# One inference step of a two-layer hybrid decoder: when the copies of the decode state are issued among the gathers of layer 1

## The chip, the cores and the metric

The kernel runs on one core of a Trainium2 chip. The metric is the device time of one execution in microseconds (us). Before the change the median of three runs is 816.68 us (815.47 to 819.44).

## The reference, cut to what matters

The step runs two layers for a prompt of 256 tokens and for eight samples of one new token each, all in float32. Layer 0 has differential attention and an indexer-sparse attention. Layer 1 has a native sparse attention (compressed blocks, selected blocks, a window of 512) and a dilated attention with three pairs of window and step, (128, 1), (512, 4) and (2048, 16). Each layer has one input projection, gates, one output projection and norms.

The outputs hold the results and the new state. For the samples, the state of the window attention and of the three dilated pairs is the old buffer shifted by the new row:

```
kd_all = [jnp.concatenate([d_bufs[2 * g], kd[g]], axis=1) for g in range(n_g)]
...
keep = lambda a, w: a[:, a.shape[1] - min(w, a.shape[1]):]
for g, (w, _) in enumerate(D_PAIRS):
    d_new += [keep(kd_all[g], w), keep(vd_all[g], w)]
```

Eight samples times eight such buffers are 64 blocks of old rows. They go unchanged from an input in device memory to an output in device memory, and no computation reads the copies. One sample's rows are 2048 KB for `d_k2` or `d_v2`, 1022 KB for `d_k1` or `d_v1`, 254 KB for `d_k0` or `d_v0`, and 255.5 KB for `c_win_k` or `c_win_v`.

## The kernel before, in words

Each engine follows one list of events, `ORDER` (built by `even_order` and `odd_order`), and does its own part of each event. TensorE (PE) carries out the projections (`rows`, `decode_rows`, lines 917 and 928), transposes (line 847), scores (1038), outputs of attention (1072) and the decode parts (1168, 1247, 1360, 1427). ScalarE (ACT) takes results out of PSUM, VectorE (DVE) does rotations, softmax parts and the decode products.

Transfers have two issuers. SyncE (SP, queue q1 in the profile) loads the weights, line 806, in chunks `win1_0` to `win1_13` for layer 1 and `wout1_0`, `wout1_1` for its output projection; the two halves of the buffer `ring` take them by turns, so that a chunk's load is issued when the one before last has been used. It also stores the new rows of prompt and samples (`out_p_...`, `out_s_... <-Z`, lines 2651 and 2657) and loads the post-norm weights (2619). At the end of layer 1 its program order is `wout1_0`, `wout1_1`, the post-norm weights, 16 stores of dilated values (line 2657), and at last `y`.

GpSimd (POOL, queue q0) issues what the decode side reads: gathers from the paged caches (`ak`, `av`, `bk`, `bv`, `ck`, `cv`; lines 814, 820, 826) and plain loads of the window and dilated state (`wk`, `wv`, `dk`, `dv`; line 810). Each waits until its buffer is free. In layer 1 their order is: ck0_0, ck0_1, ck1_0, ck1_1, dk0_0, cv_0, dk0_1, cv_1, cv_2, cv_3, dk1_0, dk1_1, wk0_0, wk0_1, dk2_0, wv_0, wv_1, dv0_0, dv0_1, dv1_0, dv1_1, dv2_0. A load `dk`, `wk`, `wv` or `dv` is 1024 KB. The last three `dv` loads lie in the half of `ring` that `win1_12` has left.

The 64 copies stand in one list, `MOVES`, in groups of four: the samples of `d_k2` and then `d_v2`, beside them those of `d_k0`/`d_v0`, `d_k1`/`d_v1`, `c_win_k`/`c_win_v`. POOL issues them too. After each gather or load it takes as many copies off the list as the table `MOVED_AFTER` (line 793) has under the gather's name, or else under its first two letters, or else none. What is left follows the last gather, `dv2_0`. A copy is cut into 16 pieces, one for each DMA engine, from memory to memory; nothing waits for it but the end of the program.

One wait matters at the end. The first product of layer 1's output projection is written into space from which SP's stores still read. So both ACT and DVE wait, ahead of that product (`out_rows` 1, 0, 0; lines 1635 and 2472), until every store of SP counted in `out0` has landed:

```
if (c, t) == (0, 0):
    ...
    eng.wait_ge(sem("post_in"), 16 * (l + 1))
    if l:
        eng.wait_ge(sem("out0"), 16 * (len(OUTS[0]) + len(OUTS[1])))
```

PE waits for `wout1_0` ahead of the same event. The last event chain after it is: ACT squares (1620), DVE weighting (2481), ACT copies of the transposed mix (1469), two products by PE of 16 matmuls each (917), the decode rows (928), the last product (917), norm and store.

Of the kernel before, what the change touches and what calls it, by code (L numbers as in the profile page):

```python
# [390 lines left out]
def build(nc, ins, outs):  # L391
    ctx = ExitStack()
    with ctx:
# [395 lines left out]
        for group in zip(moved("d_k2", 512) + moved("d_v2", 512), moved("d_k0", 512) + moved("d_v0", 512),  # L789
                         moved("d_k1", 512) + moved("d_v1", 512), moved("c_win_k", 128) + moved("c_win_v", 128)):  # L790
            MOVES += group

        MOVED_AFTER = dict(ak=1, ck=1, cv=1, dk=1, wk=1, wv=2, ak0_0=0, ak0_1=0, rows1_2=4, av7_1=3, bv_1=3, bv_3=4,
                           ck1_1=2, dk0_0=2, dk0_1=2, wk0_1=2, dk2_0=4, dk1_0=2, dk1_1=2, dv0_0=2, dv0_1=2)

        def stream(eng, name, parts):
            slot, before = place[name]
# [1872 lines left out]
        def _(pool):  # L2670
            pool.wait_ge(sem("index"), 5)
            moves = list(MOVES)
            for name, queue, parts in items:
                if queue == "pool":
                    stream(pool, name, parts)
                    for _ in range(MOVED_AFTER.get(name, MOVED_AFTER.get(name[:2], 0))):
                        if moves:
# [54 lines left out]
```

## Time and profile before

| what | value |
|---|---|
| median of three runs | 816.68 us |
| the profiled execution, its own time | 822.99 us |
| its span | 821.1 us |
| PE busy | 751.4 us, 92% |
| DVE busy | 426.0 us, 52% |
| ACT busy | 240.9 us, 29% |
| POOL busy | 165.0 us, 20% |
| DMA | 213.08 MB, mean 260 GB/s |
| q0 (POOL's transfers) | 142.55 MB |
| q1 (SP's transfers) | 69.62 MB |

Busy shares are of the span. The profiled execution's own time is 1.9 us above its span and 6.3 us above the median. In the profile MB are millions of bytes, KB are 1024 bytes. The letter q behind an engine's name means its sequencer, and L917 is line 917 of the kernel.

### The profile page before, as it was taken

To read this page: it belongs to the slowest core of one execution; us is meant where nothing else is said; L and a number is where in the kernel's file an instruction comes from. 1 tells how busy PE (TensorE), PEld (TensorE's weight loads), DVE (VectorE), ACT (ScalarE), POOL (GpSimd) and SP (SyncE) were. 2 spreads that over 40 slices of the span, in tenths; PEclk is the share of its full clock that TensorE was granted. 3 is DMA by queue.
4 is the path that set the end of the run, shared out by engine and by line. 5 is a ranking of instruction groups with operands and counts; after the bars stand their busy time and mean duration, and the time that the engine had idled before them with its cause. 6 is when DMAs were issued, how large, how long until landed. Compare 5 with 4: busy or idle time off the path is not lost.

```text
span 821.1 us, 12676 instructions
## 1 busy us (share of the span) xinstructions
PE 751.4 (92%) x4874; PEld 402.1 (49%) x4874; DVE 426.0 (52%) x958; ACT 240.9 (29%) x601; POOL 165.0 (20%) x202
## 2 busy tenths in 40 slices
PE   6989999998899799998999998899898799999896
PEld 4455545444454234433554554555554455555543
DVE  2114598999967989845244233231745425322214
ACT  6234233222213201122154323242330233232222
POOL 0523312011330333430101032410231101001000
PEclk9989999999999999998999999999999999999999
DMA  8656768889895777695595495786769977857901
GB/s 289 227 184 232 264 223 320 308 307 377 278 321 188 287 247 296 214 361 225 196 327 166 162 358 219 247 304 256 263 205 395 396 279 298 306 169 256 348 27 54
DMA packets 67828, 213.08 MB, mean 260 GB/s; under 512 B 5056, under 2 KB 28784, under 8 KB 61880
## 3 DMA queue, kind: packets, MB, share of 16 engines
q0 software_dynamic: 20320, 142.55, 47.5%
q1 hardware_dynamic: 47288, 69.62, 24.1%
q8 instruction: 39, 0.64, 0.3%
q14 instruction: 21, 0.17, 0.1%
q10 hardware_dynamic: 160, 0.11, 0.0%
HBM read 206.22 MB, written 64.68 MB: 330 GB/s over the span
## 4 chain that ended last, share of the span: by engine, by line
PE 67%; DVE 15%; DMA 7%; ACT 5%; issue 5%; POOL 1%; DVEq 0%; ACTq 0%; SPq 0%
PE psum L917 29%; PE psum L983 11%; PE psum L847 7%; PE psum L928 5%; DMA ring<-in_w_in_odd 4%; DVE SA L2344 3%; PE psum L898 2%; PE psum L1072 2%; DMA ring<-in_cache_a_v,index_a 2%; PE psum L1038 2%; DVE ring L2341 2%; PE psum L1326 2%; PE psum L1168 1%; ACT Z L1469 1%; PE psum L1360 1%
## 5 line engine op out<-in xcount | busy, mean ns | idle before, releaser
L917 PE MATMUL psum<-ring,XB 128*128 128x512 f32 (+3 forms) x760 | 326.4, 583 | 4.6 <-DMA ring<-in_w_in_odd 3.6
L917 PEld LDWEIGHTS psum<-ring,XB 128*128 128x128 f32 x760 | 142.8, 193 | 160.3 <-issue 152.4
L983 PE MATMUL psum<-Z,ring 128*128 128x512 f32 x256 | 120.6, 617 | 1.4 <-issue 1.2
L1902 DVE TENSOR_TENSOR RT<-Z,const 128x128 f32<-128x128 f32 (+6 forms) x43 | 11.5, 267 | 136.2 <-ACT Z L1559 112.3
L983 PEld LDWEIGHTS psum<-Z,ring 128*128 128x128 f32 x256 | 47.8, 195 | 61.8 <-issue 60.6
L1559 ACT ACTIVATE Z<-psum,stat 128x512 f32<-128x512 f32 (+3 forms) x38 | 24.1, 634 | 170.2 <-PE psum L917 157.0
L928 PE MATMUL psum<-ring,XB 128*8 128x128 f32 (+3 forms) x1664 | 50.2, 268 | 5.3 <-issue 3.6
L928 PEld LDWEIGHTS psum<-ring,XB 128*8 128x8 f32 x1664 | 41.6, 90 | 23.7 <-issue 22.8
L1723 ACT ACTIVATE SM<-SM,stat 128x128 f32<-128x128 f32 (+4 forms) x56 | 26.9, 480 | 71.6 <-DVE stat L2091 70.5
L1469 ACT COPY NW<-psum 128x512 f32<-128x512 f32 (+1 forms) x56 | 32.7, 583 | 47.1 <-PE psum L847 41.5
L2174 DVE MAX8 small<-KC 8x8 f32<-8x1025 f32 x32 | 38.9, 1217 | 1.6
L2176 DVE MATCH_REPLACE8 KC<-small,KC 8x1025 f32<-8x1025 f32 x32 | 38.4, 1200 | 0.0
L847 PE MATMUL psum<-const,Z 128*128 128x128 f32 (+4 forms) x220 | 30.1, 268 | 8.6 <-DVEq L2463 2.8
L1581 ACT COPY Z<-psum 8x128 f32<-8x128 f32 (+3 forms) x104 | 26.1, 251 | 37.4 <-PE psum L928 25.0
L898 PE MATMUL psum<-ring,XB 128*128 128x512 f32 (+1 forms) x72 | 32.8, 605 | 2.6 <-DMA ring<-in_w_in_even 1.5
L847 PEld LDWEIGHTS psum<-const,Z 128*128 128x128 f32 (+4 forms) x220 | 23.3, 141 | 21.5 <-issue 12.0
L847 PE MATMUL psum<-const,ring 128*128 128x128 f32 (+1 forms) x192 | 29.0, 294 | 4.0 <-ACT Z L1469 2.7
L1469 ACT COPY PT<-psum 128x256 f32<-128x256 f32 (+4 forms) x34 | 15.2, 447 | 56.0 <-PE psum L847 48.2
L1072 PE MATMUL psum<-Z,PT 128*128 128x128 f32 x168 | 25.0, 286 | 5.4 <-issue 2.5
L1072 PEld LDWEIGHTS psum<-Z,PT 128*128 128x128 f32 x168 | 21.5, 192 | 15.0 <-issue 12.6
L847 PEld LDWEIGHTS psum<-const,ring 128*128 128x128 f32 (+1 forms) x192 | 21.6, 143 | 14.7 <-issue 12.2
L814 POOL DMA_INDIRECT ring<-in_cache_a_k,index_a x11 | 10.7, 971 | 84.7 <-DVE SA L2344 75.4
(347 smaller groups left out, 902.7 us busy)
## 6 DMA issues: line engine op xcount, KB each, us to landing
ring<-in_w_in_odd SPq DMA_DIRECT2D x9, 2048.0 KB, 14.5
ring<-in_w_in_even SPq DMA_DIRECT2D x6, 2048.0 KB, 12.5
ring<-in_cmp_w SPq DMA_DIRECT2D x4, 2048.0 KB, 12.1
ring<-in_w_in_odd SPq DMA_DIRECT2D x8, 1024.0 KB, 23.0
out_s_d_k<-in_state_d_k POOLq DMA_DIRECT2D x8, 1022.0 KB
out_s_d_v<-in_state_d_v POOLq DMA_DIRECT2D x8, 1022.0 KB
Z<-in_cmp_w POOLq DMA_DIRECT2D x5, 1024.0 KB, 7.8
ring<-in_state_d_v POOLq DMA_DIRECT2D x5, 1024.0 KB, 7.5
```

The source lines that it names most:

```text
L847: return nc.tensor.transpose(out, in_, C("ident", n)[:, 0:n])
L898: mm(P.filling[:, 0:n], xT[:, k, t * 128:(t + 1) * 128], w[:, k * n:(k + 1) * n], start=k == 0, stop=False)
L917: last = mm(out[:, 0:n], xT[:, k, t * 128:(t + 1) * 128], w[:, k * n:(k + 1) * n], start=k == 0, stop=k == KT - 1)
L928: last = mm(out[32 * g:32 * g + 8, 0:q], xTs[:, k, :], w[:, k * n + g * q:k * n + (g + 1) * q], start=k == 0, stop=k == KT - 1)
L983: last = mm(out[:, h * 512:(h + 1) * 512], w[:, (r % 16) * CH + h * 128:(r % 16) * CH + h * 128 + 128], rowsT[:, at:at + 512], start=r == ...
L1072: last = mm(out[:, m * HD:(m + 1) * HD], PT[0:u["kw"], i * 128:(i + 1) * 128], u["v"][m][k], start=k == 0, stop=k == u["kt"] - 1)
L1469: copy(dst, src).then_inc(T.free, 1)
L1581: copy(z[0:8, g * q:(g + 1) * q], P.reading[32 * g:32 * g + 8, 0:q]).then_inc(s, 1)
L1723: act(x, x, ACT.Exp, scale=-1.0, bias=stat[:, (n % 2) * 4 + m:(n % 2) * 4 + m + 1], accum_out=stat[:, 64 + (n % 4) * 4 + m:65 + (n % 4) * ...
L2174: V.max(w8, x).then_inc(step, 1)
L2176: V.match_replace(x, w8, x, -BIG).then_inc(step, 1)
L2344: V.tensor_reduce(SA[:, at:at + 32], ap(slot[:, 0:1], [64, 32], [1, 64]), AX.X, add).then_inc(sem("scored"), 1)
```

## The change: what it does

Only the table is changed.

```diff
-        MOVED_AFTER = dict(ak=1, ck=1, cv=1, dk=1, wk=1, wv=2, ak0_0=0, ak0_1=0, rows1_2=4, av7_1=3, bv_1=3, bv_3=4,
-                           ck1_1=2, dk0_0=2, dk0_1=2, wk0_1=2, dk2_0=4, dk1_0=2, dk1_1=2, dv0_0=2, dv0_1=2)
+        MOVED_AFTER = dict(ak=1, ck=1, cv=1, dk=0, wk=0, wv=2, dv=2, ak0_0=0, ak0_1=0, rows1_2=4, av7_1=3, bv_1=3, bv_3=4,
+                           ck1_1=2, dk0_0=1)
```

The order of the copies stays, and so do the first 33 of them with their places, up to ck1_1. Applied by hand to POOL's order, the table puts the other 31 as follows. A group is four copies, `d_v2`, `d_v0`, `d_v1`, `win_v` of one sample.

| behind | copies before | copies after |
|---|---|---|
| dk0_0 | 2 | 1 |
| cv_0 to cv_3 | 4 | 4 |
| dk0_1, dk1_0, dk1_1 | 2 each | 0 |
| wk0_0, wk0_1 | 1, 2 | 0 |
| dk2_0 | 4 | 0 |
| wv_0, wv_1 | 2 each | 2 each |
| dv0_0, dv0_1 | 2 each | 2 each |
| dv1_0, dv1_1 | 0 | 2 each |
| dv2_0, the last gather | 0, then the 4 left | 2, then the 12 left |

Since the list is taken in order, the copies beside wv_1, dv0_0 and dv0_1 are others after the change: `d_v2`, `d_v0`; `d_v1`, `win_v`; `d_v2`, `d_v0` in place of `d_v1`, `win_v`; `d_v2`, `d_v0`; `d_v1`, `win_v`.

## Rows read from the trace of the kernel before

**Rows 1.** The page: the chain that ended last, by engine, shares of the span.
```profile
PE 67%; DVE 15%; DMA 7%; ACT 5%; issue 5%; POOL 1%; DVEq 0%; ACTq 0%; SPq 0%
```
**Rows 2.** Waits of PE, 480 to 821 us: total, times, longest us.
```profile
PE psum L917 <- DMA ring<-in_w_in_odd: 3.6, 1, 3.6
PE psum L1262 <- DVE Z L2141: 3.4, 1, 3.4
```
**Rows 3.** Timeline of PE, 628 to 660 us: start, us, what, idle before.
```profile
630.82 8.69 PE L917 MATMUL psum<-ring,XB 128*128 128x512 f32 x16
...
646.07 7.13 PE L917 MATMUL psum<-ring,XB 128*128 128x512 f32 x16 [3.57 <-DMA ring<-in_w_in_odd]
```
**Rows 4.** The chain in order of time: start us, us, what.
```profile
613.87 32.16 DMA ring<-in_w_in_odd
...
719.65 6.87 PE psum L917 x16
...
763.71 1.72 PE psum L1427 x16
...
779.16 6.88 PE psum L917 x16
...
786.14 0.70 ACT PD L1620 x2
```
**Rows 5.** DMA packets by queue, 613.9 to 646.07 us: packets, MB, share.
```profile
q0 software_dynamic: 1499, 10.76, 84.1%
q1 hardware_dynamic: 1078, 2.14, 18.3%
```
**Rows 6.** DMA packets by queue, 644 to 653 us.
```profile
q0 software_dynamic: 245, 3.61, 99.2%
q1 hardware_dynamic: 195, 0.20, 7.0%
```
**Rows 7.** A load of SP issued at 688.68 us: KB, us to landing.
```profile
ring<-in_w_in_odd SPq DMA_DIRECT2D x1, 1024.0 KB, 26.9
```
**Rows 8.** Timeline of POOL, last issues: start, us, what, idle before.
```profile
738.03 1.57 POOL L810 DMA_DIRECT2D ring<-in_state_d_v  x2 [35.50 <-PE psum L928]
750.82 0.75 POOL L810 DMA_DIRECT2D ring<-in_state_d_v  x1 [11.23 <-PE psum L1427]
751.56 1.51 POOL L2681 DMA_DIRECT2D out_s_d_v<-in_state_d_v  x3
```
**Rows 9.** Windows: stretch, us, busy by engine, PE clock, DMA share, GB/s.
```profile
644.00:653.00 9.00, 6.93 (x16) 2.96 (x16) 4.67 (x4) 0.00 (x0) 0.00 (x0) 1.00 1.07 425
...
738.00:747.00 9.00, 9.00 (x47) 6.09 (x46) 3.22 (x9) 4.11 (x10) 1.57 (x2) 1.00 0.68 235
747.00:751.00 4.00, 3.49 (x14) 0.92 (x12) 0.36 (x2) 0.95 (x2) 0.18 (x1) 1.00 0.00 0
755.00:764.00 9.00, 9.00 (x88) 4.59 (x91) 0.78 (x2) 1.40 (x5) 0.00 (x0) 1.00 1.08 400
766.00:782.00 16.00, 13.81 (x73) 8.69 (x72) 5.27 (x15) 3.63 (x7) 0.00 (x0) 0.89 1.01 378
782.00:800.00 18.00, 16.19 (x51) 7.93 (x50) 2.15 (x7) 4.40 (x10) 0.00 (x0) 1.00 0.00 0
```
**Rows 10.** Timeline of SP at the end: start, us, what.
```profile
763.77 2.21 SPq L806 DMA_DIRECT2D ring<-in_w_out_odd  x2
...
770.65 0.83 SPq L2657 DMA_DIRECT2D out_p_d_v<-Z  x2
...
777.20 2.50 SPq L2657 DMA_DIRECT2D out_s_d_v<-Z  x2
```
**Rows 11.** DMA packets by queue, 754 to 782 us.
```profile
q1 hardware_dynamic: 3757, 6.08, 59.0%
q0 software_dynamic: 304, 4.26, 41.4%
```
**Rows 12.** Windows at the drop of PE's clock.
```profile
630.00:634.00 4.00, 4.00 (x7) 1.69 (x6) 3.13 (x3) 0.17 (x1) 0.00 (x0) 0.57 0.89 287
```

## The prediction

> **What bounds the kernel now.** The chain of waits came first: PE holds 67% of it, DMA 7% [rows 1]. PE's own waits say how much of that DMA share is real: in all of layer 1 PE stood still for a transfer once, 3.6 us, beside a wait of 3.4 us for DVE [rows 2]. The timeline has its place: 3.57 us ahead of the 16 matmuls at 646.07 us [rows 3]. That load, 2048 KB of weights, was on the chain for 32.16 us [rows 4], and while it ran q0, POOL's queue, moved 10.76 MB against q1's 2.14 [rows 5]. So the copies do delay SP's loads, and there PE pays.
>
> Next to read is the end. ACT takes the first product of the last projection at 786.14 us, right behind PE's 779.16 + 6.88 [rows 4]. The wait for all of SP's stores (`out0`) does not show, because the stores have landed: the DMA engines ran at 378 GB/s up to 782 us and moved nothing from 782 to 800 [rows 9]. The slack is about 4 us. Layer 0 does not change; neither do the first 33 copies.
>
> **What is removed.** I count in MB of the profile: `d_k2`/`d_v2` 2.10, `d_v1` 1.05, `d_v0` 0.26, `win_v` 0.26; a group of four is 3.67. Between 604 and 640 us 11.0 MB of copies go (`d_v2`; `d_v0`, `d_v1`; `win_v`, `d_v2`; `d_v0`; `d_v1`, `win_v`; and the four behind dk2_0), and 0.26 MB behind cv_3 comes. The load issued at 613.87 then shares the engines with at most five plain loads of 1.05 MB. That is 7.3 MB, at 400 GB/s [rows 9] 18.3 us: it lands at 632 us at the latest, and PE wants it at 646.07 - 3.57 = 642.5. The stall of 3.57 us goes, with 10 us to spare, and nothing else is late in its place: the wait of 3.4 us for DVE stands before it and is no transfer. Bounds: at most 3.6 us, since no other transfer is waited for; at least 0, if another wait takes over. I take -3.6 us. That POOL issues fewer copies between its loads is worth nothing: each is 0.5 us [rows 8], on an engine that then waits for a buffer.
>
> **What moves inside 685 to 711 us.** wv_1, dv0_0 and dv0_1 now carry 2.36, 1.31 and 2.36 MB, before 1.31, 2.36 and 1.31: 1.05 MB more, 2.6 us at 400 GB/s. Behind it is the load issued at 688.68, which landed 26.9 us later [rows 7], at 715.6; PE wants it at 719.65 [rows 4]. 715.6 + 2.6 = 718.2, so nothing, with 1.4 us left. The bounds are 0 and 3 us, the latter if SP's share is thinner than I reckon.
>
> **What is added at the end.** POOL issues dv1_0 and dv1_1 at 738.03 and dv2_0 at 750.82 [rows 8]. Before, 2.10 MB moved from 738 to 747 (235 GB/s over 9 us), the engines stood idle from 747 to 751, and the last group of four went at 400 GB/s until 764 [rows 9]. That was all off q0 before SP began at 763.77 [rows 10]. After, still in the clock of before:
> - From 738: two loads, 2.10 MB, and four copies (`d_v1`, `win_v`, `d_v2`, `d_v0`), 3.67 MB. The first data come 1.7 us after the issue (2.10 MB at 400 GB/s are 5.3 us, the last landed at 747 at the latest). 5.77 MB take 14.4 us: 754.1.
> - dv2_0, 1.05 MB: 756.7. PE works on the two loads before it at 763.71 [rows 4] and on it after that, so it is in time, and so is dv1_1, 3 us later than before.
> - Two copies, 1.31 MB, and twelve, 11.00 MB: 12.31 MB, 30.8 us: 787.5 us. POOL's 14 issues are 7 us of an idle engine.
>
> SP issues `wout1_0` and `wout1_1` at 763.77 and the stores from 770.65 to 779.7 [rows 10], in all 6.08 MB [rows 11]. The price is what these wait for. While q0 has copies, its packets are large and q1's small: from 644 to 653 us q1 sent 195 packets with 0.20 MB and q0 245 with 3.61 [rows 6]. From 765.5 to 787.5 q1 then gets 0.5 MB, or twice that with its larger packets. But for the last store the share hardly matters, as the engines are busy throughout: what q1 gains, q0 loses. I add 6.08 MB at 378 GB/s [rows 9], 16.1 us, to the 787.5: the last store lands at 803.6 us.
>
> The Trainium skill (DMA: Bandwidth & Descriptors, Queues, rings and completion order) says that an engine takes the queues in turn, a packet from each, so a share goes by packets and not by bytes. By that rule the two queues do not split the bandwidth evenly, and rows 6 agree (195 packets beside 245, 0.20 MB beside 3.61); it takes chance from the even-split rival below. Its section on bandwidth (Where 436 GB/s comes from) puts the memory's limit for a core near 358 GB/s; by it, as an estimate, the last store would land about 6 us later still. The 400 GB/s of rows 9 for copies alone is above that, and the measurement decides.
>
> `wout1_0`, 2.10 MB, lands near 791. PE's first product runs then, to about 798, below the wait for the stores and so for nothing. ACT and DVE come to their wait for `out0` and stand until 803.6. Behind ACT's wait are its squares and the copies of the transposed mix; for those PE waits, and with it the whole rest. Against 786.14 that is 17.5 us. If the copies run at the 425 GB/s of 644 to 653 [rows 9], they end 2.8 us earlier; if SP's issues are held up by the backlog, it is some 3 us more. I take 17.5, with bounds of 14.5 and 21.
>
> **Clock.** After the DVE wait PE's granted clock was 0.57 for 4 us [rows 12], part of it at the lower of its two levels, 1.2 GHz; 16 matmuls took 8.69 in place of 7.13 us [rows 3]. Now PE will idle for more than 10 us and again for 5 ahead of its last 32 and 16 matmuls. One such drop is 1.6 us. Nothing, or two, are the bounds (0 and 3.2); I take 1.6.
>
> **Sum.** -3.6 + 17.5 + 1.6 = +15.5 us: the span goes from 821.1 to 836.6, the execution's own time from 822.99 to 838.5. The median of before is 6.3 us below its profiled execution; the same difference on the median gives 816.68 + 15.5 = 832.2 us. That all copies have landed at 787.5, long before the end, means the wait for them costs nothing.
>
> **Rivals.**
> 1. Even split: q0 and q1 share by bytes, 200 GB/s each from 765.5. SP's 6.08 MB take 30.4 us, to 795.9, while q0 is still busy. The stall is 9.8: -3.6 + 9.8 + 1.6 = +7.8, 824.5 us. For: where q0's packets were of the loads' size, q1 kept up better (2.14 of 12.9 MB, rows 5). Against: rows 6. Chance 0.15.
> 2. Not slower: SP's transfers go ahead of the copies, or the copies' writing costs the engines so little beside them that the stores still land by 786 - 3.6. Then the end costs nothing, only the 3.57 us at 646 counts, and the time is 813.1, or a little less if waits for weights upstream of ACT shrink too. It decides at 4 us of slack: SP must get 6.08 MB through in 20 us, 300 of the 400 GB/s. For: the last group did not harm SP when it ended just before. Against: rows 5 and 6. Chance 0.12.
> 3. A second stall: the load for 719.65 comes up to 3 us late, and SP's stores behind it push `win1_13`. The time is 835. Chance 0.13.
>
> **How the numbers follow.** My forecast has 0.6, within 828 to 836. The range must reach over the even split and the second stall: 821 to 838. Outside are rival 2 and a small part of the rest. A change of 0.5%, 4.1 us, is about the least that a measurement of this kernel can tell from none. Rival 2 lies at -3.6 us, on the edge: I give 0.05 to faster and 0.08 to within 0.5%, the other 0.87 to slower.
>
> **What would show it.** In the trace after: no wait of PE for `w_in_odd` near 640 us, and that load in under 20 us (right: the removal); 14 copies issued within 8 us of dv2_0; q0 busy to about 784 (3.6 earlier than 787.5); in the ten us before that q1 below 60 GB/s; the stores landing at about 800; PE's first wait at the last projection for `w_out_odd`, near 10 us; ACT's L1620 not directly behind PE's product but some us later, released by a store; a clock of about 0.5 at the start of the last 32 matmuls. Wrong if q1 runs at 200 GB/s or more beside the copies, or if ACT follows PE at once.

## The result, and the profile after

The kernel after takes 845.23 us, median of 4 runs (843.42 to 852.86), against 818.06 us (815.47 to 819.59) for the kernel before on the same chip: ratio 1.0319, interval 1.0276 to 1.0363, or 22.6 to 29.7 us more. Slower was predicted; the time lies above the range of 821 to 838 us.

The profiled execution of after took 843.42 us with a span of 841.6, mean clock 0.968; before, 822.99, 821.1 and 0.978. First the chain that ended last, by engine, and the granted clock in 40 slices of 21 us. DMA's share is down from 7% [rows 1] to 4%, and SP's own queueing (SPq) is new with 4%. The 5 is the only slice near the clock's lower level, 1.2 GHz:

```profile
PE 65%; DVE 15%; ACT 5%; issue 5%; SPq 4%; DMA 4%; POOL 1%; DVEq 0%; ACTq 0%
...
PEclk9989999999999999999999999999999999999599
```

The waits, with total, times and longest us. PE from 480 us: the one for `w_in_odd` [rows 2] is gone, one of 25.3 us for `w_out_odd` has come, the one for DVE is as it was. ACT from 700 us: a wait of 35.8 us for a store, which before did not show.

```profile
PE psum L917 <- DMA ring<-in_w_out_odd: 25.3, 1, 25.3
PE psum L1262 <- DVE Z L2141: 3.3, 1, 3.3
```

```profile
ACT PD L1620 <- DMA out_s_d_v<-Z: 35.8, 1, 35.8
```

PE's timeline: start, duration, what, idle before. The instruction that waited at 646.07 [rows 3] now starts at 639.57 with no idle time. The 16 matmuls of L1427 at 756.93 are those of 763.53 before (the chain in [rows 4] has them from 763.71). I use their start as a mark, B, which stands ahead of everything at the end that the 12 last copies delay. Before, the first product of the last projection came 15.5 us behind B; now it is 39.8 us behind, and takes 9.57 us instead of 7.03. First before, then after:

```profile
639.43 1.93 PE L928 MATMUL psum<-ring,XB 128*8 128x128 f32 x64
...
664.15 1.93 PE L928 MATMUL psum<-ring,XB 128*8 128x128 f32 x64
...
763.53 1.90 PE L1427 MATMUL psum<-ring,PD 128*32 128x512 f32 x16
...
778.99 7.03 PE L917 MATMUL psum<-ring,XB 128*128 128x512 f32 x16
...
789.44 14.00 PE L917 MATMUL psum<-ring,XB 128*128 128x512 f32 x32
```

```profile
636.67 1.93 PE L928 MATMUL psum<-ring,XB 128*8 128x128 f32 x64
...
639.57 7.03 PE L917 MATMUL psum<-ring,XB 128*128 128x512 f32 x16
...
657.56 1.93 PE L928 MATMUL psum<-ring,XB 128*8 128x128 f32 x64
...
756.93 1.90 PE L1427 MATMUL psum<-ring,PD 128*32 128x512 f32 x16
...
796.70 9.57 PE L917 MATMUL psum<-ring,XB 128*128 128x512 f32 x16 [25.34 <-DMA ring<-in_w_out_odd]
...
809.97 14.00 PE L917 MATMUL psum<-ring,XB 128*128 128x512 f32 x32
```

The chain at the end: SP queues for 28.72 us at L2619 (the load of `post_norm`), then comes a store of `d_v`, then ACT's take, its first reading of the first product (L1620). The 32 matmuls behind it take as long as before:

```profile
764.00 28.72 SPq L2619
...
801.61 4.91 DMA out_s_d_v<-Z
...
806.68 0.70 ACT PD L1620 x2
...
810.04 13.93 PE psum L917 x32
```

SP's timeline says where the time went. In [rows 10] the stores were issued from 770.65; now SP stands for 33.37 us at the load of 759.35, while the two loads ahead of it wait beside the copies, and the stores start at 792.77. (The chain counts only the last 28.72 us of it, from a signal of L1437 at 764.00. Before, SP was through with this load at 768.50, ahead of L1437, so it is not what SP waits for.)

```profile
757.17 2.13 SPq L806 DMA_DIRECT2D ring<-in_w_out_odd  x2
759.35 33.37 SPq L2619 DMA_DIRECT2D NW<-in_post_norm  x1
...
792.77 2.14 SPq L2657 DMA_DIRECT2D out_p_d_v<-Z  x2
...
801.21 0.79 SPq L2657 DMA_DIRECT2D out_s_d_v<-Z  x2
```

The windows of the end (stretch, us, busy by engine, PE clock, DMA share, GB/s). A window counts a packet whole where it starts, so short ones swing: 786 to 790 has few starts, but packets from before were still under way. Over 754 to 793 the DMA engines are full, at 336 GB/s where [rows 9] had 400 and 378, and the clock is at its lower level while PE has no work.

```profile
754.00:793.00 39.00, 14.96 (x152) 9.05 (x150) 6.04 (x17) 6.15 (x15) 0.00 (x0) 0.76 0.98 336
...
774.00:786.00 12.00, 0.00 (x0) 0.00 (x0) 0.00 (x0) 0.00 (x0) 0.00 (x0) 0.51 1.01 345
786.00:790.00 4.00, 0.00 (x0) 0.00 (x0) 0.00 (x0) 0.00 (x0) 0.00 (x0) 0.50 0.65 192
...
793.00:805.00 12.00, 8.30 (x14) 3.70 (x15) 0.00 (x0) 0.00 (x0) 0.00 (x0) 0.64 0.90 340
807.00:820.00 13.00, 10.89 (x34) 5.17 (x33) 1.70 (x4) 4.08 (x10) 0.00 (x0) 1.00 0.00 0
```

The queues from 759 to 786 us (packets, MB, share of 16 engines): packet for packet the two are nearly even, 343 to 299 (154 of the 343 are of 4 bytes), and by bytes 14 to 1. SP's queue gets 0.61 MB in 27 us, 23 GB/s.

```profile
q0 software_dynamic: 343, 8.59, 94.2%
q1 hardware_dynamic: 299, 0.61, 7.0%
```

**The difference in three parts.** Measured between fixed instructions, the spans (841.6 - 821.1 = 20.5 us) split so: 2.8 us less ahead of dk0_0, the first gather that the change touches (530.60 against 533.36 us); this is the same work, with fewer drops of the clock. 3.8 us less in the stretch that held the stall, from the L928 ahead of it to the next (20.9 us for 24.7). Nothing between it and B, 99.4 us in both. From B to the end of the span, which I call the tail, 84.7 us for 57.6: 27.1 more. -2.8 - 3.8 + 27.1 = 20.5.

### The profile page after: what moved, and what is told of

It reads as the page before. It is cut to its first block, busy times and chain, and to the rows that moved or that the text cites. A ratio compares the mean times of both kernels' runs of the same rounds, so it can differ in the third digit from the quotient of the medians.

```text
span 841.6 us, 12676 instructions
## 1 busy us (share of the span) xinstructions
PE 749.3 (89%) x4874; PEld 400.7 (48%) x4874; DVE 426.0 (51%) x958; ACT 240.9 (29%) x601; POOL 164.3 (20%) x202
## 4 chain that ended last, share of the span: by engine, by line
PE 65%; DVE 15%; ACT 5%; issue 5%; SPq 4%; DMA 4%; POOL 1%; DVEq 0%; ACTq 0%
PE psum L917 29%; PE psum L983 10%; PE psum L847 7%; PE psum L928 5%; SPq L2619 3%; DMA ring<-in_cache_a_v,index_a 3%; DVE SA L2344 2%; PE psum L898 2%; PE psum L1038 2%; PE psum L1072 2%; DVE ring L2341 2%; PE psum L1326 1%; PE psum L1168 1%; PE psum L1247 1%; ACT Z L1469 1%
## 5 line engine op out<-in xcount | busy, mean ns | idle before, releaser
L917 PE MATMUL psum<-ring,XB 128*128 128x512 f32 (+3 forms) x760 | 326.9, 583 | 26.3 <-DMA ring<-in_w_out_odd 25.3
L928 PE MATMUL psum<-ring,XB 128*8 128x128 f32 (+3 forms) x1664 | 50.1, 268 | 5.3 <-issue 3.6
L928 PEld LDWEIGHTS psum<-ring,XB 128*8 128x8 f32 x1664 | 41.4, 90 | 23.7 <-issue 22.6
L1072 PEld LDWEIGHTS psum<-Z,PT 128*128 128x128 f32 x168 | 21.4, 191 | 14.8 <-issue 12.5
L814 POOL DMA_INDIRECT ring<-in_cache_a_k,index_a x11 | 10.7, 970 | 84.7 <-DVE SA L2344 75.4
```

The lines of the kernel that those rows point to most:

```text
L917: last = mm(out[:, 0:n], xT[:, k, t * 128:(t + 1) * 128], w[:, k * n:(k + 1) * n], start=k == 0, stop=k == KT - 1)
L928: last = mm(out[32 * g:32 * g + 8, 0:q], xTs[:, k, :], w[:, k * n + g * q:k * n + (g + 1) * q], start=k == 0, stop=k == KT - 1)
L1072: last = mm(out[:, m * HD:(m + 1) * HD], PT[0:u["kw"], i * 128:(i + 1) * 128], u["v"][m][k], start=k == 0, stop=k == u["kt"] - 1)
```

## The experiments

**e1, the kernel before again.** No edit.

> The kernel before, unchanged: how much of the 6 us between its profiled execution and its median lies in stretches that the change does not touch. The trace of after is 2.8 us ahead of that of before already at dk0_0 (530.60 against 533.36 us), ahead of the first edit. Theory: the profiled execution of before was a slow one of its kind, and this one has a span of 814 to 818 us, with dk0_0 near 530.5, the stall of 3.6 us for w_in_odd near 643 still there, and copies of the last group that end about 11 us after they begin (755.3 to 766.4 before). Rival: the 2.8 us belong to the kernel of before, and the span is again near 821.

815.78 us, span 814.0 (814 to 818 expected), clock 0.984. dk0_0 came at 524.9 us, not near 530.5. The stall is there, with half of the expected length:

```profile
637.33 7.13 PE L917 MATMUL psum<-ring,XB 128*128 128x512 f32 x16 [1.77 <-DMA ring<-in_w_in_odd]
```

So the stall varies by 2 us between executions of one kernel, and the removal is worth 2 to 3.8 us. The tail is 59.2 us (57.6 in the first execution); the 32 matmuls took 15.70 us for 14.00. The part ahead of dk0_0, the same list of instructions in all kernels of this study, varies more: to one matmul near 490 us it takes 483.5 to 494.9 us, with 6.8 us at the lower clock in the quickest and 30.7 us in the slowest (e9, whose copies have small packets here too). Single times therefore mislead, and I compare the stretch behind B.

**e2, the removal alone.** The kernel before, with the 14 copies that would move left out where they stood.

```
+ LEFT_OUT = dict(dk0_0=1, dk0_1=2, dk1_0=2, dk1_1=2, wk0_0=1, wk0_1=2, dk2_0=4)
- for _ in range(MOVED_AFTER.get(...)):
+ for k in range(MOVED_AFTER.get(...)):
      if moves:
          dst, src = moves.pop(0)
+         if k < LEFT_OUT.get(name, 0):
+             continue
- sp.wait_ge(sem("moved"), 16 * len(MOVES))
+ sp.wait_ge(sem("moved"), 16 * (len(MOVES) - 14))
```

> The kernel before with the 14 copies beside dk0_0 (one), dk0_1, dk1_0, dk1_1, wk0_0, wk0_1 and dk2_0 left out altogether (their rows of the state are not written), and all other copies where they were. What the removal is worth by itself. My theory: the 3.6 us stall for w_in_odd and no more, 813.5 to 815.5 against 818. Rival: it is worth nothing here (another wait takes over), 818; or more than the one wait shows, 808 to 812.

812.31 us (808.66 to 821.44, 4 runs); ratio 0.9899, interval 0.9788 to 1.0009. PE does not wait for `w_in_odd`, the stretch takes 20.9 us, and no other wait came in its place. By the traces the removal gains the stall and no more, 2 us against e1 and 3.8 against the first execution; the ratio is too wide to say more.

**e3, after without its last 12 copies.**

```
- for dst, src in moves:
-     pool.dma_start(dst, src).then_inc(sem("moved"), 16)
+ moves.clear()
- sp.wait_ge(sem("moved"), 16 * len(MOVES))
+ sp.wait_ge(sem("moved"), 16 * (len(MOVES) - 12))
```

> The kernel after with the 12 copies behind the last gather left out (their rows are not written). If the whole loss is the backlog at the end, this is at the level of the removal alone, 813.5 to 815.5 against 818 for before and 845 for after. If the copies beside wv, dv0 and dv1 cost anything by themselves, it stays at 816 to 822.

815.93 us (10 runs); 0.9928, interval 0.9886 to 0.9970. ACT's take is 22.6 us behind B, as before (after: 49.8), and the tail 59.2, as in e1. So the whole loss sits in these 12 copies. What the change does between 685 and 711 us costs nothing.

**e4 and e11, the 12 copies behind the stores.** POOL issues them once SP's last store of `out0` has landed; no work is left out. e11 is the same kernel once more, in 5 rounds.

```
+ pool.wait_ge(sem("out0"), 16 * (len(OUTS[0]) + len(OUTS[1])))
  for dst, src in moves:
      pool.dma_start(dst, src).then_inc(sem("moved"), 16)
```

> The kernel after, with POOL waiting, between dv2_0's two copies and the last 12, until all of SP's stores (out0) have landed. The same copies, all of them, but behind SP's transfers and not ahead of them. Theory (order in the DMA engines is the whole price): SP's stores land as in the kernel before, PE waits for nothing, the 11 MB then run from about 776 to 810 us beside no other load, end before the last y, and the time is 813.5 to 815.5. At 330 GB/s the copies take 33 us, at 400 27.5 us: the trace tells which. Rival (amount, not order): the engines are too busy either way, or the copies end after the last y, and the time stays above 820.

> e4 again beside e10, in more rounds: 0.990 to 0.998 of before, the same as e10 within 0.3%.

e4: 817.33 us (10 runs), 0.9938, interval 0.9897 to 0.9978. e11: 818.55 us (12 runs), 0.9963, interval 0.9928 to 0.9998. The copies are the same, with the same bytes, and the tail is 60.0 and 60.3 us for 84.7: what cost the time is that they stand ahead of SP's transfers, not that they come late. ACT's take follows PE's product at once, 21.4 us behind B in both executions. (The profiled execution of e4 was the longest of its ten, 823.41 us; that of e11 took 814.06, and behind B the two agree.) Here e4's POOL and ACT:

```profile
781.22 1.46 POOL L2682 DMA_DIRECT2D out_s_d_v<-in_state_d_v  x3 [30.55 <-DMA out_s_d_v<-Z]
```

```profile
783.00 0.60 ACT L1620 ACTIVATE PD<-psum 128x512 f32<-128x512 f32 x1 [7.47 <-PE psum L917]
```

e4 also measures the copies nearly by themselves. SP's loads and stores alone ran at 392 GB/s over 15 us. The 11.00 MB of copies took from 782.4 to 817.9 us, 310 GB/s. The second window happens to show the same rate: it has 2 us without a transfer in it and 0.75 MB of SP's. The copies end 3.7 us ahead of the span's end.

```profile
764.00:779.00 15.00, 12.61 (x75) 7.64 (x74) 5.27 (x15) 3.64 (x7) 0.00 (x0) 1.00 1.04 392
...
780.00:818.00 38.00, 30.80 (x199) 15.52 (x197) 11.35 (x30) 9.40 (x26) 5.79 (x12) 0.94 0.93 310
```

**e5, after without the stores of the dilated values.** It takes away the stores that ACT waits for.

```
+ del OUTS[1][EARLY1:]
```

> The kernel after with SP's last 16 stores (the new rows of the dilated values, out_p_d_v and out_s_d_v) left out, so that they are not written and out0 no longer waits for them. Which of the two waits of the end is the price. The prediction's theory: the wait for the stores alone, PE's first product being free below it; then the time falls by 10 us or more from 845. Rival, by the trace of after (PE waited 25.3 us for w_out_odd, its first product ran at the lower clock level, 9.57 us, and ended at 806.3, the last store landed at 806.56): both end together, so that taking the stores away gives back 0 to 2 us, 843 to 845.

835.98 us (3 runs) against 819.42; 1.0201, interval 1.0128 to 1.0273. By the times alone 9 us came back and the store wait would look like a third of the loss. The trace says otherwise: ACT's take is 49.1 us behind B for 49.8, the tail 84.0 for 84.7. Most of the rest of the profiled execution's lower time lies ahead of every edit: to the matmul near 490 us it took 483.8 us, that of after 489.5. ACT now stands for PE:

```profile
799.06 0.60 ACT L1621 ACTIVATE PD<-psum 128x512 f32<-128x512 f32 x1 [35.16 <-PE psum L918]
```

So two waits end together behind the backlog: `wout1_0` with PE's product, and the stores. Taking the stores away gives 0.7 us, as the rival had it (0 to 2). No run takes `wout1_0` away.

**e6, each copy as 128 pieces.** It was meant to make the copies' packets small.

```
- m = (new - 1) * n // 16
- return [(bass.AP(..., [[m, 16], [1, m]]), bass.AP(..., [[m, 16], [1, m]]))
+ m = (new - 1) * n // 128
+ return [(bass.AP(..., [[m, 128], [1, m]]), bass.AP(..., [[m, 128], [1, m]]))
```

> The kernel after with every copy cut into 128 pieces in place of 16 (16 KB, 8 KB and 2 KB in place of 128 KB, 64 KB and 16 KB). Same bytes, same order. Theory (a share goes by packets): q1 gets several times its 25 to 35 GB/s beside them, w_out_odd lands 5 to 12 us earlier, and since POOL's bytes still go before the last stores, the time falls only in part, to 832 to 842. If the large pieces are also what holds the copies to 330 GB/s, q0 is done sooner and it is 825 to 835. Rival (a share goes by bytes, or size does not matter): 845, w_out_odd lands as before.

845.04 us (3 runs); 1.0308, interval 1.0234 to 1.0381, tail 84.3 us. The queues from 759 to 786 us show packets of the old size (8.31 MB in 334): pieces that touch had been joined again. The experiment therefore tests nothing of the question. As a second execution of the same transfers it helps: here ACT's take was released by PE's product, not by a store, 49.4 us behind B.

```profile
q0 software_dynamic: 334, 8.31, 91.0%
q1 hardware_dynamic: 286, 0.59, 7.3%
```

**e9, the same with pieces that do not touch.** Neighbours in the order of the pattern are now 16 * m elements apart.

```
- [[m, 16], [1, m]]
+ [[m, 16], [16 * m, 8], [1, m]]      (m = (new - 1) * n // 128)
```

> The kernel after with each of a copy's 16 parts cut again into 8 pieces that do not touch in memory, so that they can't be merged (in e6 the pieces were merged back: its trace has the same packets of 64 KB). Packets of 16 KB, 8 KB, 2 KB and 2 KB in place of 64, 64, 16 and 16 KB, same bytes, same order. Theory (shares go by packets): per group an engine has some 36 packets in place of 9, so q1 gets about 100 GB/s in place of 25 to 35 beside the copies, w_out_odd lands near B+25 in place of B+39.8 (B: start of PE's work on dv1_0 and dv1_1), PE's wait for it is about 10 us in place of 25. The last store still comes behind all of POOL's bytes, so ACT takes the first product near B+46 to B+50 as in the kernel after (B+49.8), and the time falls by 0 to 4 us only: 841 to 845. Rival (shares go by bytes or by queue, whatever the packets): w_out_odd near B+39 as before. Rival (large packets hold the copies to 330 GB/s): the copies end 5 to 8 us earlier and the time is 836 to 839.

854.69 us (4 runs) against 822.29; 1.0409, interval 1.0360 to 1.0459. All the expectations of the time missed, and so did that of `w_out_odd`: it landed 43.1 us behind B, not 25. The queues from 768 to 804 us:

```profile
q0 software_dynamic: 1128, 9.72, 80.8%
q1 hardware_dynamic: 1157, 2.34, 19.8%
```

Again nearly a packet for a packet, and with q0's at 8.6 KB, SP's queue gets 65 GB/s for 23. The share goes by packets, as predicted. It did not help: both queues together moved 12.06 MB in 36 us, 335 GB/s, the backlog still has to drain, and the copies ended 45.1 us behind B for 36.3. ACT's take is 54.7 us behind B for 49.8, the tail 92.8 us; 3.0 us of the tail's 8.1 are the last 32 matmuls, 17.00 us for 14.00.

**e7 and e8, one group and two groups of four ahead of the stores.** The dose between e4 (none) and after (three). A group is 3.67 MB.

```
  for k, (dst, src) in enumerate(moves):
+     if k == 4:                      (e8: k == 8)
+         pool.wait_ge(sem("out0"), 16 * (len(OUTS[0]) + len(OUTS[1])))
      pool.dma_start(dst, src).then_inc(sem("moved"), 16)
```

> The kernel after with the last 12 copies split: 4 at once, 8 behind the wait for SP's stores. Dose of the backlog: one group of 3.67 MB. Theory: each group puts 11 us on q0 (330 GB/s, 755.3 to 766.4 in the trace of before) and the price starts when q0's end passes the slack. With two copies beside each of dv1_0, dv1_1, dv2_0 and one group, q0 ends near 770 in the frame of before: 3 to 9 us above the kernel without the group (e4, 0.9938 of before). Rival (by 400 GB/s): 0 to 4 us above it.

> The same with 8 at once and 4 behind the wait: two groups, 7.33 MB. Theory: 14 to 20 us above e4, that is 11 above e7 and 9 to 11 below the kernel after. Rival (by 400 GB/s, 9.2 us for each group): 9 to 13 us above e4.

e7: 820.02 us (10 runs); 1.0013, interval 0.9972 to 1.0054. e8: 832.15 us (4 runs); 1.0124, interval 1.0044 to 1.0205. ACT's take in e7, e8 and after:

```profile
777.72 0.60 ACT L1620 ACTIVATE PD<-psum 128x512 f32<-128x512 f32 x1 [11.34 <-DMA out_s_d_v<-Z]
```

```profile
795.64 0.60 ACT L1620 ACTIVATE PD<-psum 128x512 f32<-128x512 f32 x1 [24.70 <-PE psum L917]
```

```profile
806.68 0.60 ACT L1620 ACTIVATE PD<-psum 128x512 f32<-128x512 f32 x1 [35.81 <-DMA out_s_d_v<-Z]
```

Behind B (751.25, 757.00 and 756.93 us) that is 26.5, 38.6 and 49.8 us; with no group 21.4. From one to two groups 12.2 us, from two to three 11.1: 3.67 MB at 301 to 330 GB/s, as expected from the rate and not from 400 (9.2 us). The first group costs only 5.1 us, because the slack takes the rest. By the times e7 is about 6 us above e4 (3 to 9 expected) and e8 about 15 (14 to 20); e8 is some 16 us below after, where 9 to 11 were expected, but behind B it is 11.1. SP stood at the load L2619 for 2.1 us with no group ahead (e3), 10.2 in e7, 20.8 in e8 and 33.4 in after.

**e10, one group back behind dk2_0, the other copies behind the stores.** e4 with `dk2_0=4` in the table.

```
-                            ck1_1=2, dk0_0=1)
+                            ck1_1=2, dk0_0=1, dk2_0=4)
```

> A version meant to beat both: the table of after with four copies put back behind dk2_0 (where the engines have little to do until wv_0, 25 us later, and the next SP load has 25 us until PE wants it), and the last 8 behind the wait for SP's stores. Theory: no wait for w_in_odd near 640, tail from B as in e4 (57 to 60 us against 84.7 in after), copies done about 11 us before the end where e4's end 4 us before it; 0.985 to 0.995 of before, the same as e4. Rival: the four copies delay the load issued near 639 or the one for 664, and it is 1 to 3 us above e4.

819.14 us (12 runs); 0.9962, interval 0.9926 to 0.9997, where 0.985 to 0.995 was expected. No wait for `w_in_odd` appeared. The copies end at 797.6 us of a span of 811.9, 14.3 us ahead of the end for e4's 3.7; tail 58.1 us for 60.0 and 60.3. In the times it is not told from e11 (0.9963). These versions are a little faster than before, 0.4 to 0.6%, with intervals that just leave out 1 in e10 and e11, and by the ratios 3.5% faster than after (0.9963 / 1.0319; the two were not run side by side).

## Why the prediction was right, and where its size was wrong

**The removal: right.** -3.6 us was predicted, -3.8 measured, no wait came in its place (e2). The packets of the load issued at 611.11 ended at 627.5 us, within the 20 us that were set as a sign. In e1 the same stall was 1.8 us, so the agreement to 0.2 us is partly luck.

**685 to 711 us: right.** 99.4 us from the stretch to B before and after; e3 shows that nothing is lost there. The second stall (rival 3) did not come.

**How the queues share: right.** q1 got 23 GB/s beside the copies; predicted was under 60. The even split (rival 1) is refuted by 343 packets beside 299 with 14 times the bytes, and by e9, where smaller packets raised q1's share. "What q1 gains, q0 loses" held in e9 too: q1's share rose and the copies ended later. Rival 2, not slower, fell with it; but its condition, SP's transfers ahead of the copies, is what e4 builds, and there its price (about -3.6 us) is what was measured (0.9938 and 0.9963 are -5.1 and -3.0 us).

**The end: right in mechanism, wrong in size. This is the step that failed.** Predicted: the last store at 803.6, 40.1 us behind B (763.53). Measured: 801.61 + 4.91 = 806.5, 49.6 us behind B, 9.5 later. In its own terms:
- dv2_0's packets ended at 754.2, 2.7 us ahead of B; predicted 756.7, 6.8 ahead. 4.1 us.
- The copies behind it, 12.31 MB, ended at 793.2: 39.0 us, 316 GB/s, for the 30.8 us predicted at 400. 8.2 us.
- SP's remainder took 13.3 us for 16.1, since 2.03 MB of its 6.08 had gone beside the copies. -2.8 us. 4.1 + 8.2 - 2.8 = 9.5.

So the mis-sized term is the rate of 400 GB/s for the copies, and it was read wrongly from [rows 9]. The window 755 to 764 counts packets whole where they start, and most of the group's last 16 large packets were still under way at its end. The group was not off q0 before SP began at 763.77, either, as the prediction has it. The same window up to the landing, then the queue in it (the group's 3.67 MB and the end of the load ahead of it):

```profile
755.00:767.00 12.00, 12.00 (x110) 6.46 (x110) 0.78 (x2) 2.92 (x10) 0.00 (x0) 1.00 0.99 347
```

```profile
q0 software_dynamic: 199, 3.83, 87.7%
```

The group ran from 755.3 to 767.0 us (its last packets start at 766.4): 3.67 MB in 11.7 us, 312 GB/s. With that the trace of before would have given 12.31 MB in 39.5 us, 8.7 us more than was taken, and 5.77 MB in 18.5 us, 4.1 more. The bounds (14.5 to 21) went wrong with it. Their faster end came from 425 GB/s, a rate that the engines did reach for some 10 us with copies, but over no whole group; nothing slower than 400 was allowed for. e7 and e8 confirm the rate as a dose, e4 as 310 GB/s.

The Trainium skill's figure for a core's memory limit (DMA: Bandwidth & Descriptors, Where 436 GB/s comes from), near 358 GB/s, which the prediction set aside for the 400 of its window, would as an estimate have come closer, with about 6 of the 9.5 us. But the traces do not bear it out as a limit for all: SP's loads and stores alone ran at 392 GB/s in e4, above it, and whole groups of copies at 310 to 316, below. It depends on what is moved.

**"PE's product below the store wait, and so for nothing": half right.** `wout1_0` was to land near 791, 27.5 us behind B; it landed 39.8 behind it, at 796.7, and PE's product, at 9.57 us, ended 0.3 us ahead of the last store. e5 shows the two tied: without the stores 0.7 us came back, and in e6 and e8 it was the product that released ACT. PE's wait was to be near 10 us and was 25.3. Of the cause behind both the prediction allowed "some 3 us" for SP's issues. SP stood for 33.37 us at one load, and issued the stores from 792.77. Most of that took no time of its own, as the engines were full. But the 4.05 MB left at 793.2 would have taken 10.7 us at 378 GB/s and took 13.3, so up to 2.6 us may lie in the late issue of the stores; no run separates this.

**Clock: mechanism there, price hidden.** PE, idle from 771.3 us, was at the lower level from 774.3 to 801.6. That cost the first product 2.5 us (9.57 for 7.03), which ended just below the store wait. The last 32 matmuls took 14.00 us at a clock of 1.00, as before. The +1.6 us did not come there: in all the tail grew by 27.1 us, and ACT's take alone moved by 27.1 (49.75 - 22.61). Nor is such a drop the change's own: in e1, the kernel before, the 32 matmuls took 15.70 us.

**The sum by its steps:** -3.6 became -3.8, 0 stayed, +17.5 became +27.1, +1.6 became 0; with the 2.8 us that lie ahead of the change, 20.5 for 15.5 in the profiled executions. By the medians it is 27.2 us. The profiled execution of before took longer than the median (822.99 for 818.06), and had more drops of the clock in its first part; without these 2.8 us the difference is -3.8 + 27.1 = 23.3, in the interval of 22.6 to 29.7. So of the 13.0 us between the predicted median (832.2) and the measured one (845.23), the traces explain 23.3 - 15.5 = 7.8; 1.4 is the new median of before, and 3.8 us stay unexplained, within the spread of single executions (the profiled one of after was the shortest of its four).

What stays open: why copies from memory to memory run slower over a whole group than loads, though not in every stretch, and what makes the stall at `w_in_odd` 3.6 us in one execution and 1.8 in another.

## What to carry to other kernels

Before work is moved behind the last item in issue order, ask which transfers still share the DMA engines there, and add the bytes ahead of each gate at the rate of a whole transfer from its start to its landing, never at that of a window inside it. In this kernel, background copies that nobody waits for belonged behind the last transfer that somebody waits for: one wait on the stores' semaphore (e4) turned +3.2% into -0.4 to -0.6%. When one wait is taken away and nothing moves, look for a second that ends with it, and compare fixed stretches of the trace where executions differ by more than the effect.

## What the runs showed of the hardware

- Copies from memory to memory moved 310 GB/s over 35.5 us (e4) and 312 to 316 over whole groups (before, after), though the engines moved 425 in a stretch of 9 us with copies in it [rows 9]; SP's loads and stores moved 378 to 392. A packet of 64 KB took 2.4 us (median) from 640 to 680 us of before, 3.1 us in the backlog of after and 3.0 to 3.1 in e4's.
- Cutting the copies' packets to an eighth raised the other queue's rate from 23 to 65 GB/s and made the kernel slower (1.0409 against 1.0319); part of that is the clock (3.0 us).
- Pieces of an access pattern that touch were joined into the same packets (e6: 334 packets of 8.31 MB, after: 343 of 8.59).
- SP stood at the issue of one load for 2.1, 10.2, 20.8 and 33.4 us with 0, 1, 2 and 3 groups of copies in the other queue, and all its later stores stood behind it.
- PE, idle from 771.3 us, was at a clock of 0.50 from 774.3 to 801.6, and the product that began at 796.70 took 9.57 us for 7.03.
